# Retention with another order of products and kept gates, side blocks 512 wide, and macaron products on modulated input

## What is computed

```python
# block one, layer 0 (retention) and layer 1 (neighbourhood attention)
m_lat = split(silu(c) @ ada_w[i] + ada_b[i], 6)           # modulation vectors, latent
m_ctx = split(silu(c_ctx) @ ada_w[i] + ada_b[i], 6)       # and context
q, k, v, g = split(a @ w_in)                               # 4 heads, dk 256, dv 512
o = bidirectional_scan(q, rope(k) * dk ** -0.5, v, decay)  # as masked scores here
y = (silu(g) * o * rsqrt(mean(o * o) + eps)) @ w_out
h = layer_norm(ALPHA * h + m[2] * y)
f = (silu(gate) * up) @ w2, gate, up = split(modulate(h, m[3], m[4]) @ w13)
# block two, per layer: macaron feed-forward, hybrid mixer, macaron feed-forward
mod = silu(c_2) @ ada_w_2[l] + ada_b_2[l]                  # 9 vectors
u = rmsnorm(h) * g * (1 + sc) + sh
h = h + 0.5 * gt * ((silu(u @ wg) * (u @ wu)) @ wd)
```

## Time and profile before

| what | before |
|---|---|
| median of 3 runs | 3343.29 us |
| profiled execution, its own time | 3334.63 us |
| its span | 3333.3 us |
| busy: PE, DVE, ACT, POOL | 93%, 64%, 36%, 8% |
| mean granted TensorE clock | 0.943 |
| DMA | 524.77 MB, 157 GB/s over the span |

### The profile page before, as it was taken

The page is one execution under the profiler, slowest core; times in us unless marked ns, Lnnn a source line. Parts: engine busy times, 40 slices in busy tenths (PEclk is TensorE's granted clock), DMA queues, the critical chain, the costliest instruction groups (busy, mean ns, idle before and its releaser), DMA issues.

```text
span 3333.3 us, 55236 instructions
## 1 busy us (share of the span) xinstructions
PE 3109.6 (93%) x23574; PEld 2900.9 (87%) x23574; DVE 2133.2 (64%) x3166; ACT 1198.8 (36%) x1533; POOL 275.8 (8%) x283
## 2 busy tenths in 40 slices
PE   7899999799999799899999989999999998999999
PEld 4777878699999777899899989889999998897998
DVE  5676776776677677555665854466656575545664
ACT  2112122344444233444444411444444442134543
POOL 5000000110102021101001020000000101000101
PEclk9889999799999899899999989999999998999999
DMA  7253443488999656466556612336575562222654
GB/s 271 89 178 106 154 142 94 147 247 242 253 249 281 220 165 207 133 178 190 150 159 165 171 32 71 99 117 177 157 198 156 162 173 68 65 84 82 181 161 126
DMA packets 746225, 524.77 MB, mean 157 GB/s; under 512 B 19242, under 2 KB 711660, under 8 KB 745852
## 3 DMA queue, kind: packets, MB, share of 16 engines
q1 hardware_dynamic: 741852, 516.18, 53.9%
q0 software_dynamic: 4128, 5.06, 0.5%
HBM read 520.07 MB, written 2.94 MB: 157 GB/s over the span
## 4 chain that ended last, share of the span: by engine, by line
PE 46%; issue 18%; DVE 10%; ACT 8%; DMA 1%; POOL 1%; SPq 0%; DVEq 0%; ACTq 0%; POOLq 0%
PE bank L454 11%; PE bank L456 11%; PE bank L455 11%; ACT weights_hi L424 6%; PE bank L1296 2%; DVE weights_lo L434 1%; ACT mac_gate L1843 1%; DVE mac_prod L1876 1%; DVE side_sums L541 1%; PE bank L2211 1%; PE bank L2223 1%; PE bank L2219 1%; PE bank L562 1%; DVE mac_gate L1872 1%; PE bank L1316 1%
## 5 line engine op out<-in xcount | busy, mean ns | idle before, releaser
L434 DVE TENSOR_TENSOR weights_lo<-weights_raw,weights_hi 128x2048 fp32r<-128x2048 f32 (+3 forms) x414 | 852.8, 2061 | 388.6 <-ACT weights_hi L424 388.4
L424 ACT ACTIVATE weights_hi<-weights_raw 128x2048 fp32r<-128x2048 f32 (+3 forms) x414 | 709.1, 1714 | 737.2 <-PE bank L456 663.1
L454 PE MATMUL bank<-norm_in_hi,weights_hi 128*128 128x258 f32 x1408 | 406.6, 289 | 16.1 <-DVE mac_prod L1873 10.4
L456 PE MATMUL bank<-norm_in_hi,weights_lo 128*128 128x258 f32 x1408 | 399.1, 283 | 0.0
L455 PE MATMUL bank<-norm_in_lo,weights_hi 128*128 128x258 f32 x1408 | 398.5, 283 | 0.0
L454 PE MATMUL bank<-ffn_in_hi,weights_hi 128*128 128x256 f32 x1184 | 348.0, 294 | 19.5 <-DVE ffn_in_lo L1088 8.6
L455 PE MATMUL bank<-ffn_in_lo,weights_hi 128*128 128x256 f32 x1184 | 344.0, 291 | 0.0
L456 PE MATMUL bank<-ffn_in_hi,weights_lo 128*128 128x256 f32 x1184 | 343.9, 290 | 0.0
L454 PE MATMUL bank<-mix_in_hi,weights_hi 128*128 128x256 f32 x960 | 286.2, 298 | 15.5 <-DVE conv_in L2090 6.4
L454 PEld LDWEIGHTS bank<-norm_in_hi,weights_hi 128*128 128x128 f32 x1408 | 267.5, 190 | 28.4 <-issue 27.3
L455 PE MATMUL bank<-mix_in_lo,weights_hi 128*128 128x256 f32 x960 | 278.7, 290 | 0.0
(11 more groups left out here) (422 smaller groups left out, 6932.8 us busy)
## 6 DMA issues: line engine op xcount, KB each, us to landing
weights_raw<-in_ffn_w SPq DMA_DIRECT2D x132, 512.0 KB, 5.5
weights_raw<-in_w_in SPq DMA_DIRECT2D x120, 512.0 KB, 5.1
side_weights<-in_ada_w SPq DMA_DIRECT2D x86, 576.0 KB, 4.2
weights_raw<-in_ffn_wg SPq DMA_DIRECT2D x88, 512.0 KB, 4.0
weights_raw<-in_ffn_wu SPq DMA_DIRECT2D x88, 512.0 KB, 5.3
...
```

Source lines behind the costliest of these rows:

```text
L424: k.s.activation(k.w_hi[s % HIGHS][:, 0:n], k.raw[s % RING][:, 0:n], ACT.Copy).then_inc(*k.hi.up())
L434: k.v.tensor_tensor(k.w_lo[s % RING][:, 0:n], k.raw[s % RING][:, 0:n], k.w_hi[s % HIGHS][:, 0:n].bitcast(F32), ALU.subtract).then_inc(*k.l ...
L454: k.te.matmul(out, l[0], r[0], start=first, stop=False)
L456: return k.te.matmul(out, l[1], r[0], start=False, stop=last)
```

## The change

1. Retention has one list of slabs, `RET_SLABS`: the first q, then per head k v v g g, the q of the next head, and o four times. Scores stand before the first g, values before the second, and the sums of squares are 16 matmuls of one column inside the second g's product (`pe_ret_sums`). 1/rms is made on 128x4, and four small matmuls (`pe_ret_spread`) bring it back to 128x512. The masks are made beside the v slabs, the silu of all four gate chunks is kept in four tiles, and DVE multiplies them in one run (`dve_ret_gated`) after the second g.
2. Side blocks of block one are 512 wide: 20 instead of 16. Retention runs 14 of them, three steps per slab, with two accumulators instead of one; q0 runs 5 (40 steps, two per slab in up slabs 16 to 19), q1 the last one and four of block two (40 steps); q4 has 32 steps of block two (22 and 10), which it had not. Finishes of q0 and q1 come after up slabs 9, 17, 21 and down slabs 7 and 15.
3. In the macarons, up slabs from `LATE` = 6 on multiply the normed and modulated input `xn` (256 columns), which POOL, ACT and DVE make during slabs 0 to 5; their DVE part is one product, and ACT takes silu straight from the bank.
4. A few small tiles have other places; the layer norm vectors of layer 1 are made later.

```diff
-SIDE1 = 768
+SIDE1 = 512
+SIDE_L1 = 8
+SIDE_M2 = 20
+RET_BLOCKS = 14
+RET_STEPS = 3
...
+def retention_order():
+    out = [(0, "q", 0)]
+    for hd in range(RET_H):
+        out += [(hd, "k", 0), (hd, "v", 0), (hd, "v", 1), (hd, "g", 0), (hd, "g", 1)]
+        if hd + 1 < RET_H:
+            out.append((hd + 1, "q", 0))
+        out += [(hd, "o", n) for n in range(4)]
+    return out
+
+
+RET_SLABS = retention_order()
+RET_FINISH = {(KD * b + KD - 1) // RET_STEPS + 1: b for b in range(RET_BLOCKS)}
...
     steps = []
+    for b in range(SIDE_M2):
+        layer = int(b >= SIDE_L1)
+        c0 = (b - SIDE_L1) * SIDE1 if layer else 2 * D + b * SIDE1
+        steps += [(a["ada_w"][layer], i, c0, SIDE1, (0, KD)) for i in range(KD)]
...
+    if b < SIDE_M2:
+        return k.side_acc[0][:, (b % 2) * 2 * SIDE1:(b % 2 + 1) * 2 * SIDE1]
+    return k.side_acc[1 - b % 2][:, 0:SIDE2]
...
-        k.v.wait_ge(k.side_sum.h, b - 1 if b > 4 * RET_H else b)
+        k.v.wait_ge(k.side_sum.h, max(b - 1, 0))
...
-    free = i - 2 if at >= 3 else (WIDE if i >= WIDE else 0)
+    free = i - 2 if at >= 3 else (SIDE_M2 * KD if i >= SIDE_M2 * KD else 0)
...
-RET_SIDES = [4, 4, 4, 4, 3, 3, 2, 3, 3, 2]
-RET_ENDS = {1: 0, 3: 1, 6: 2, 9: 3}
+def ret_turn(k, g):
+    return k.t0 + g + sum(at < g for at in RET_FINISH)
...
+def ret_steps(g):
+    return max(min(RET_STEPS, RET_BLOCKS * KD - g * RET_STEPS), 0)
...
+def pe_ret_sums(k, hd):
+    te = k.te
+    te.wait_ge(*k.ret_squared.at(4 * hd + 4))
+    te.wait_ge(*k.ret_taken.at(4 * hd + 4))
+    for tt in range(4):
+        for c in range(4):
+            m = te.matmul(k.AB[0][:, tt:tt + 1], flat(k.sq[:, 2 * c:2 * c + 2, :])[:, tt * P:(tt + 1) * P],
+                          k.ones[:, 0:1], start=c == 0, stop=c == 3)
+    m.then_inc(*k.ret_summed.up())
+
+
+def pe_ret_spread(k, hd):
+    k.te.wait_ge(*k.rms_inverted.at(hd + 1))
+    for tt in range(4):
+        m = k.te.matmul(k.AB[1][:, tt * P:(tt + 1) * P], k.small[:, tt:tt + 1].broadcast_to([P, P]), k.ident, start=True,
+                        stop=True)
+    m.then_inc(*k.rms_spread.up())
...
 def pe_retention(k):
+    te = k.te
+    for g, (hd, what, n) in enumerate(RET_SLABS):
+        if what == "g" and n == 0:
+            pe_ret_scores(k, hd)
+        if what == "g" and n == 1:
+            pe_ret_values(k, hd)
+        w = pe_slab(k)
+        bank = pe_turn(k)
+        if g == 0:
+            m = chunk_by_chunk(k, [b[:, :] for b in bank], w, k.am, slice(0, 2 * T), KD, lambda n: k.am_lo.at(2 * n + 2))
+        elif what in "qkg":
+            for c in range(2):
+                m = feature_major(k, bank[c][:, :], w, c * P, k.am, slice(0, 2 * T))
+                if what == "g" and n == 1 and c == 0:
+                    pe_ret_sums(k, hd)
...
+        m.then_inc(*k.used.up())
+        if what == "g" and n == 1:
+            pe_ret_spread(k, hd)
+        if g in RET_FINISH:
+            pe_side_finish(k, RET_FINISH[g])
...
+def dve_ret_gated(k, hd):
+    v, x = k.v, ret_gates(k)
+    v.wait_ge(*k.rms_spread.at(hd + 1))
+    for c in range(5):
+        if c < 4:
+            v.tensor_tensor(k.ret_o[:, c, :], k.ret_o[:, c, :], k.AB[1][:, :], ALU.mult).then_inc(*k.dve.up())
+            v.wait_ge(*k.ret_silu.at(4 * hd + c + 1))
+            v.wait_ge(*k.dve.now())
+            v.tensor_tensor(x[c], x[c], k.ret_o[:, c, :], ALU.mult).then_inc(*k.ret_gated.up())
+        if c:
+            v.wait_ge(*k.ret_zhi.at(4 * hd + c))
+            v.tensor_tensor(k.ret_zz[1][:, c - 1, :], x[c - 1], k.ret_zz[0][:, c - 1, :].bitcast(F32),
+                            ALU.subtract).then_inc(*k.ret_z.up())
...
 def dve_retention(k):
+    v = k.v
+    for g, (hd, what, n) in enumerate(RET_SLABS):
+        bank = k.GB[ret_turn(k, g) % 2]
+        sides = ret_steps(g)
+        if what == "v" and n == 0:
+            dve_ret_masks(k, hd)
+        if what == "g" and n == 0:
+            dve_ret_probs(k, hd)
+        if what == "g" and n == 1:
+            for c in range(4):
+                dve_ret_taken(k, hd, c)
+                if c < sides:
+                    dve_side(k)
+            sides = 0
+        dve_lo(k)
+        for _ in range(sides):
+            dve_side(k)
+        if what in "qk":
+            dve_ret_rope(k, hd, what, bank)
...
+        if what == "g":
+            if n == 1:
+                small = k.small[:, 0:4]
                 v.wait_ge(*k.ret_summed.at(hd + 1))
-                v.tensor_scalar(k.stat[0][:, :], k.AB[0][:, :], 1.0 / RET_DV, RMS_EPS, ALU.mult, ALU.add).then_inc(
+                v.tensor_scalar(small, k.AB[0][:, 0:4], 1.0 / RET_DV, RMS_EPS, ALU.mult, ALU.add).then_inc(
                     *k.variance_ready.up())
                 v.wait_ge(*k.root_taken.at(hd + 1))
-                v.reciprocal(k.stat[0][:, :], k.stat[0][:, :]).then_inc(*k.dve.up())
-                v.wait_ge(*k.dve.now())
-                v.tensor_tensor(k.ret_o[:, :, :], k.ret_o[:, :, :], bc(k.stat[0][:, :], 4), ALU.mult).then_inc(*k.dve.up())
...
+            v.wait_ge(*k.ret_silu.at(4 * hd + 2 * n + 2))
+            v.memset(k.small[:, 60:61], 0.0).then_inc(*k.ev.up())
+            if n == 1:
+                dve_ret_gated(k, hd)
...
+        sides = Sides(RET_BLOCKS + 5 * q, [1] * 16 + [2] * 4 + [1] * 2, [1] * 14 + [0] * 2)
...
+    sides = Sides(RET_BLOCKS + 18, [1] * KF, [1] * 10 + [0] * 6)
...
-            m = feature_major(k, bank[c][:, 0:T + 2], w, c * P, x, slice(0, T + 2))
+            if i < LATE:
+                m = feature_major(k, bank[c][:, 0:T + 2], w, c * P, x, slice(0, T + 2))
+            else:
+                m = feature_major(k, bank[c][:, 0:T], w, c * P, k.xn, slice(0, T),
+                                  ready=(lambda n: (k.norm_lo if n % 2 else k.xn_lo).at(n // 2 + 1)) if i == LATE and c == 0 else None)
             if i == 1 and c == 0:
...
+        if i < LATE:
+            s.wait_ge(*k.gate_scaled.at(i + 1))
+            s.activation(g, g, ACT.Silu, bias=k.shifted[:, c:c + 1]).then_inc(*k.gated.up())
+            s.wait_ge(*k.prod_ready.at(i + 1))
+        else:
+            s.wait_ge(*k.used.at(i + 1))
+            if i < LATE + 2:
+                s.wait_ge(*k.prod_ready.at(i - 1))
+            else:
+                s.wait_ge(k.ev.h, k.t0 + i - 1)
+            s.activation(g, k.GB[(k.t0 + i) % 2][0][:, 0:T], ACT.Silu).then_inc(*k.gated.up())
+            s.wait_ge(k.ev.h, k.t0 + i + 1)
         s.activation(k.mid[0][:, i, :], k.prod[i % 2][:, :], ACT.Copy).then_inc(*k.mid_hi.up())
         act_hi(k)
+        for n in (2 * i, 2 * i + 1) if 2 * i < KD else ():
+            sc, bi = (k.mods2[:, layer, at + n:at + n + 1] for at in (sh + KD, sh))
+            s.wait_ge(*k.times_rms.at(n + 1))
+            s.activation(k.xn[0][:, n, :], k.sq[:, n, :], ACT.Identity, scale=sc, bias=bi)
+            s.activation(k.xv[:, n % 4, :], k.sq[:, n, :], ACT.Identity, scale=sc, bias=bi).then_inc(*k.norm_hi.up())
     for i in range(4 * KD // 2):
         act_hi(k)
         if i % 4 == 1:
             s.wait_ge(*k.h_out.at(i // 4 + 1))
             act_chunk(k, i // 2, following)
...
+        if i >= LATE:
+            v.wait_ge(*k.gated.at(i + 1))
+            v.tensor_tensor(x, g, bank[1][:, 0:T], ALU.mult).then_inc(*k.ev.up())
+            v.wait_ge(k.ev.h, turn + 1)
+            v.wait_ge(*k.mid_hi.at(i + 1))
+            v.tensor_tensor(k.mid[1][:, i, :], x, k.mid[0][:, i, :].bitcast(F32), ALU.subtract).then_inc(*k.mid_lo.up())
+            continue
...
+        if 1 <= i <= KD // 2:
+            n = 2 * i - 1
+            v.wait_ge(*k.norm_hi.at(n + 1))
+            v.tensor_tensor(k.xn[1][:, n, :], k.xv[:, n % 4, :], k.xn[0][:, n, :].bitcast(F32), ALU.subtract).then_inc(
+                *k.norm_lo.up())
...
 def pool_macaron(k):
+    g, rstd = k.g, k.stat[0][:, 0:T]
+    g.wait_ge(*k.affine.at(1))
+    for n in range(KD + 2):
+        if n < KD:
+            g.tensor_tensor(out=k.sq[:, n, :], in0=k.hid[:, n, :], in1=rstd, op=ALU.mult).then_inc(*k.times_rms.up())
+        if n >= 2 and n % 2 == 0:
+            i = n - 2
+            g.wait_ge(*k.norm_hi.at(i + 1))
+            g.tensor_tensor(out=k.xn[1][:, i, :], in0=k.xv[:, i % 4, :], in1=k.xn[0][:, i, :].bitcast(F32),
+                            op=ALU.subtract).then_inc(*k.xn_lo.up())
     pool_squares(k, 1)
```

519 lines of the change are left out of this document (248 added, 271 removed).

## The result

The changed kernel takes 3313.4 us, the median of 4 runs (3296.4 to 3316.7), against 3346.9 of the kernel before beside it (4 runs, 3340.8 to 3351.0). The ratio over all runs is 0.9891 (that of the two medians is 0.9900), with a 95% interval from 0.9853 to 0.993: 23 to 49 us faster. The forecast was 3319, in a range from 3294 to 3340. The profiled execution of after is its slowest, 3316.7 with a span of 3315.3; that of before, 3334.6, was faster than all four of its others, so between the two traces only 18.0 us lie.

A forecast was written before the change was run, and what follows sets the result against it. TensorE, busy 93% of the span, was taken as the bound, with DVE pacing some retention slabs. Retention -33, q0 -4, q1 +16, q4 +16 and macarons -19 sum to -24: 3319 us, range 3294 to 3340.

The forecast's parts named there:

- The step on the waits: Retention: TensorE's waits fall from 54.5 us to about 34, mostly behind finishes among o slabs, for -20.
- Clock. ... I take -6: Retention: of 45 us lost to the slow clock, 6 come back; bounds -25 and +15.
- 5.3 and 2.1: q0 and q1, each: four up slabs with two steps cost +5.3 us, a third up-loop finish about +2.1.
- -6 for the beginning: q0's beginning: the change of width, which holds SP for 21.5 us, leaves this place, giving -6 us.
- -3 for the end: q0's end: smaller side steps remove some 3 us of stall before q1 from a weight transfer.
- 22 x 0.54: q4: 22 up slabs go from 5.70 to 6.24 us each through DVE's loop, +11.9 us.
- Two finishes in the up loop at 2.1, and two in the down part that mostly lie beside other work: +4: q4: four added side finishes cost 4 us in all, those in the down part mostly hidden.
- the 8 us taken off for contention: Macarons, slabs 0 to 5: DVE low parts slowed beside POOL cost 2 us in each of four, +8.
- DVE's chain behind the second g: Rival, retention: DVE's run of work keeps stalls at 54 us and takes all the gain; 3349 to 3364 us, chance 0.09.
- POOL and DVE lock each other: Rival, macarons: POOL instructions hold DVE's loop and eat up the gain; 3338 us, chance 0.14 together with the fourth rival.
- Side steps nearly free: Rival: q1's slabs arrive in time, q4 costs 8, retention gains 45 with a better clock; 3285 us, chance 0.13.
- The change does less than it says: Rival, macarons: `xn` late at slab 6 by the whole gain; 3338 us, chance 0.14 together with the second rival.

The follow-up runs named there:

- e11: Kernel with all finishes apart and the change of width at retention's end, plus no doubled side steps in q0's and q1's up slabs: 3224.0 us, ratio 0.9638.
- e3: Changed kernel with finishes in q0, q1 and q4 taking no turn of the banks, except the last of each: 3268.4 us, ratio 0.9784.
- e6: Changed kernel with retention's side steps spread by the load of the slab instead of three everywhere: 3276.6 us, ratio 0.9814.
- e7: Changed kernel with finishes taking no turn of the banks in the feed-forwards (but for the last of each) and in retention too: 3228.6 us, ratio 0.9687.

## Why the prediction was right, and where it was off

**The total was right, from terms that missed in both directions.** The forecast of -24 lies beside -18 between the two traces and -33.5 between the medians. The terms were off by -10 (retention), +8 (q0), +2 (q1), +7 (attention), +9 (q4) and -10 (macarons), and these cancel to +6. So the total came closer than its terms, and that closeness is luck; what was right by its mechanism is the waits in retention, the loops of q4, the change of width in q1 and the gross gain of the macarons.

**Retention.** The step on the waits was right: 34 us were laid out by hand and 33.6 are there. The step "Clock. ... I take -6" was too small. TensorE's own busy time fell by 23 us (from 516.93 + 10.77 to 504.70), where passes and clock together were to give 13. Half of the 22 us less that it was busy at the low clock is 11, against 6; the other 12 are against 7 for its own passes. The clock's 11 are what is left of 20.6 us won at scores and finishes and 10.2 lost again at the o slabs. I had looked for the cause in the one-column matmuls. For the changed kernel the runs put most of it on the idle gap beside them: with the gaps gone and all columns kept, the low clock of retention fell from 106 to 44 us, and with all but one column of each finish gone and the turns kept it stayed at 106. That in the kernel before it was the wait ahead of a finish, and not the finish, is argued from this and not shown by a run.

**q0.** The doubled steps cost what they should in their own slabs (7.2 and 7.6 us against 5.9 and 6.24 without them, e11). As a whole the up products, from the first to the last on DVE, grew from 138.0 to 141.6 us, and what follows, with the third finish in it, from 71.2 to 72.6, where 5.3 and 2.1 were forecast. What failed is "-6 for the beginning": putting the change of width back at the end of retention changes q0 by 0.3 us. The 21.5 of the earlier trace rows was a wait of a queue that had a lead. "-3 for the end" failed too: the stall before q1's first product was 3.0 us and is 2.2, and as it stands behind the last finish of q0, whose turn no run took away, its cause stays open.

**q1.** Right to 2 us as a sum, from parts that missed both ways: the up products grew by 11.6 us (133.6 to 145.2) where 13.9 were forecast, and what follows them by 6.8 (68.7 to 75.5) where 2 were. With the turns gone (e3) the latter is 68.6 again. The odd term was right: 6.5 forecast for the change of width, 6.7 seen in one interval, 7.4 back when it was undone.

**q4.** "22 x 0.54" was right: intervals of 6.24, as forecast. "Two finishes in the up loop at 2.1, and two in the down part that mostly lie beside other work: +4" was the mis-sized term, and its second half above all. The up products grew by 14.7 us (119.7 to 134.4), where 16.1 were forecast. The part behind them grew by 10.3, where nothing was; before, and then after:

```profile
1511.40:1589.10 77.70, 66.98 (x557) 66.54 (x555) 42.48 (x64) 32.30 (x37) 12.39 (x14) 0.93 0.68 195
...
1512.20:1600.20 88.00, 76.33 (x594) 75.83 (x592) 56.80 (x76) 32.69 (x37) 17.41 (x14) 0.87 0.79 226
```

Two finishes there are 4.1 us of columns, the gap behind one is 1.1, and of the 10.2 us of low clock behind them some half, 5.1, is lost: together the 10.3. In the whole of q4 the gaps are 3.7, 2.6 and 1.1 us, and with the turns of the four finishes gone and all columns kept (e3) q4 is 15.2 us shorter, or 12 against the mean of its four profiles.

**Attention.** It was forecast unchanged, and its +6.7 is no effect of the change that a run here shows: with that code it took 295.2 to 308.7 us in the other profiles, under 300 where it was at the low clock for 55 to 61 us and over 306 where for 75 to 82. The code before shows the same spread: 301.4, 307.1 and 308.4 us.

**Macarons.** The gross gain was right (27 forecast, 28.7 measured); the 8 us taken off for contention were wrong. I had priced it by a DVE instruction that came second. The low part at 612.90 of the earlier trace rows started while this instruction of POOL was running:

```profile
612.65 0.92 POOL L1013 TENSOR_TENSOR stat<-stat,stat 128x256 f32<-128x256 f32 x1
```

The low part took 0.53 us more than usual, and the one of POOL at 613.72, which came behind it, took 2.61. In the macarons POOL comes second, and has time. The loop itself did not run at 5.70 from slab 8 on, as the prediction had it, but at 4.91 until slab 11 and at 5.69 after that (5.76 in one macaron).

**The rivals.** *DVE's chain behind the second g*: the stalls that it foretold are there, though not at their old size, and it takes two things for them. Less DVE work at these slabs halves them (e6), and once finishes take no turn, one wait of 2.2 us is left with all of DVE's work in place (e7). *POOL and DVE lock each other*: the lock is there, its price is not. *Side steps nearly free*: refuted in q4. *The change does less than it says*: `xn` was in time at slab 6, and at slab 5 it is 4.8 us late, so there was one slab of room. What I did not have among them is the one that counts: that a small job in a ring of two buffers costs the pipeline a whole slab of lead.
